# Prompt attention in a two-layer hybrid decoder: eight fill products ahead of the scores, and rotary operands padded with zero rows from 32 to 128

## The reference, cut to what matters

```python
s = (jnp.einsum('bqhr,bkr->bhqk', qa, c_kv) + jnp.einsum('bqhd,bkd->bhqk', qr, k_rope)) * scale
s = jnp.where(k_pos[None, :] <= qp[:, None], s, -jnp.inf)
p = jax.nn.softmax(s, axis=-1)
return jnp.einsum('bhqk,bkr->bqhr', p, c_kv)
```

## Time and profile before

| quantity | value |
|---|---|
| runs of the kernel before | 2146.13, 2148.97, 2151.54 us (median 2148.97) |
| the profiled execution: its own time | 2145.22 us |
| the profiled execution: span of its instructions | 2143.1 us |
| TensorE busy in the span | 1848.7 us, 86% |
| DVE, ACT, POOL busy | 759.5, 350.2, 66.1 us |
| mean granted TensorE clock | 0.911 of full |
| prompt stage of layer 0 | 489.7 to 560.2 us |
| prompt stage of layer 1 | 1544.3 to 1614.8 us |

### The profile page before, as it was taken

The page is one execution under the profiler, slowest core; times in us unless marked ns, Lnnn a source line. Parts: engine busy times, 40 slices in busy tenths (PEclk is TensorE's granted clock), DMA queues, the critical chain, the costliest instruction groups (busy, mean ns, idle before and its releaser), DMA issues. The chain is left out here.

```text
span 2143.1 us, 22565 instructions
## 1 busy us (share of the span) xinstructions
PE 1848.7 (86%) x8114; PEld 1088.9 (51%) x8114; DVE 759.5 (35%) x1560; ACT 350.2 (16%) x524; POOL 66.1 (3%) x68
## 2 busy tenths in 40 slices
PE   4999999889889959988479999997998898599883
PEld 2666657456446634433236666674574475343231
DVE  2243357563223342211324234475631242332113
ACT  1013212141101021110001312122311201211000
POOL 0000000000000001111000000000000000011110
PEclk8999999896999979999779999997979999699996
DMA  7565422323364179999366652223235631999982
GB/s 291 184 228 187 138 93 79 118 72 108 119 216 167 69 315 373 422 423 421 120 267 215 220 176 98 102 79 130 68 109 167 216 122 58 370 418 423 423 350 75
DMA packets 107127, 441.05 MB, mean 206 GB/s; under 512 B 19394, under 2 KB 54498, under 8 KB 79746
## 3 DMA queue, kind: packets, MB, share of 16 engines
q1 hardware_dynamic: 79442, 408.63, 50.4%
q10 hardware_dynamic: 18352, 20.40, 3.0%
q0 software_dynamic: 9216, 10.51, 1.4%
HBM read 433.70 MB, written 28.84 MB: 216 GB/s over the span
## 5 line engine op out<-in xcount | busy, mean ns | idle before, releaser
L367 PE MATMUL ps<-s_proj_and_h,w_in_tiles 128*128 128x320 f32 x1280 | 354.4, 438 | 8.3 <-PEq L203 8.3
L367 PEld LDWEIGHTS ps<-s_proj_and_h,w_in_tiles 128*128 128x128 f32 x1280 | 243.9, 192 | 123.4 <-issue 26.7
L177 PE MATMUL ps<-s_proj_and_h,w_in_tiles 128*128 128x320 f32 x960 | 290.8, 452 | 1.2 <-ACT s_proj_and_h L187 1.2
L2036 PE MATMUL ps<-s_proj_and_h,t_ex_xf 128*64 128x512 f32 x1024 | 244.0, 632 | 32.6 <-DMA s_proj_and_h<-w_gate_up 30.9
L177 PEld LDWEIGHTS ps<-s_proj_and_h,w_in_tiles 128*128 128x128 f32 x960 | 185.0, 198 | 88.4 <-issue 25.8
L2036 PEld LDWEIGHTS ps<-s_proj_and_h,t_ex_xf 128*64 128x64 f32 x1024 | 82.9, 146 | 189.9 <-issue 189.9
L1742 PE MATMUL ps<-s_proj_and_h,w_merge 128*128 128x320 f32 x512 | 138.3, 433 | 3.8 <-PEq L1664 3.8
L1742 PEld LDWEIGHTS ps<-s_proj_and_h,w_merge 128*128 128x128 f32 x512 | 97.1, 190 | 45.1 <-issue 4.9
L2060 PE MATMUL ps<-w_down_slots,t_ex_hf 128*64 128x512 f32 x512 | 116.9, 598 | 2.5 <-DVE t_ex_hf L2107 1.0
L2105 DVE TENSOR_TENSOR t_ex_hid<-t_ex_hid,ps 128x256 f32<-128x256 f32 x32 | 13.5, 421 | 254.4 <-ACT t_ex_hid L2131 254.4
L1972 POOL DMA_INDIRECT rt_h_tm<-h_rows,t_ex_token x32 | 33.9, 1060 | 1635.0 <-DMA h_rows<-rt_h_tm 810.8
(11 more groups left out here) (424 smaller groups left out, 2012.4 us busy)
## 6 DMA issues: line engine op xcount, KB each, us to landing
s_proj_and_h<-w_gate_up SPq DMA_DIRECT2D x64, 2048.0 KB, 29.9
w_in_tiles<-w_in SPq DMA_DIRECT2D x140, 512.0 KB, 3.6
w_down_slots<-w_down SPq DMA_DIRECT2D x64, 1024.0 KB, 30.9
w_mod_panels<-w_mod SPq DMA_DIRECT2D x32, 1024.0 KB, 7.3
page_keys<-pages_k SPq DMA_DIRECT2D x128, 192.0 KB, 3.3
s_proj_and_h<-w_mod SPq DMA_DIRECT2D x16, 1024.0 KB, 12.3
w_merge<-w_branch SPq DMA_DIRECT2D x16, 1024.0 KB, 4.9
page_values<-pages_v ACTq DMA_DIRECT2D x96, 128.0 KB, 2.8
```

The lines of the kernel that those rows point to most:

```text
L177: mm = pe.matmul(K.ps[:, self.BANKS[i % 2], 0:T], self.win[:, j, k, :], K.h[:, k, :], start=(k == 0), stop=(k == KD - 1))
L367: mm = pe.matmul(K.ps[:, n % BANKS, 0:T], win[:, j, k, :], K.h[:, k, :], start=(k == 0), stop=(k == KD - 1))
L2036: mm = pe.matmul(K.ps[rows, GU, :], xf[:, k, rows], K.gate_up[:, j, k, :], start=(k == 0), stop=(k == KD - 1))
```

## The change

Three things are edited.

1. The rotary operands have 128 partitions. `K.krope` is [128, 320] and cleared once at the start of the program by POOL; `A.qr` is [128, 8, 320], and POOL clears its partitions 32 to 127 in the project stage of each layer (two memsets). All writers still write partitions 0 to 31. The rotary products of both attentions now contract over 128 rows, 96 of which are zeros.
2. In the prompt stage the 32 fill products stand at other places: 8 ahead of the first scores and 4 ahead of score(1, 0), fewer behind score(1, 1).
3. ACT's four `F.copy` calls in that stage move accordingly.

```diff
+        @block.gpsimd                                   # in mla_project_stage
+        def _(pool):
+            nc.gpsimd.memset(A.qr[ROPE:2 * ROPE], 0.0)
+            nc.gpsimd.memset(A.qr[2 * ROPE:P], 0.0).then_inc(s("qr_cleared"), 1)
+            pool.wait_ge(s("qr_cleared"), 1)
...
+            F.products(pe, 8)                           # TensorE, mla_prompt_stage
             score(0, 0)
             score(0, 1)
+            F.products(pe, 4)
             score(1, 0)
             turn(0)
             turn(1)
             F.products(pe, 4)
             pe.wait_ge(s("pr_pT_copied"), 2)
             score(1, 1)
             value(0, 0, 0)
+            F.products(pe, 4)
+            value(0, 1, 1)
             F.products(pe, 6)
-            value(0, 1, 1)
-            F.products(pe, 8)
             turn(2)
             turn(3)
-            F.products(pe, 8)
+            F.products(pe, 4)
             value(1, 0, 3)
             turn(4)
             turn(5)
-            F.products(pe, 6)
+            F.products(pe, 2)
             value(1, 1, 5)
...
-        qr_b = K.proj[0:ROPE, XBC0:XBC0 + 2, 0:NB * NSAMP // 2].rearrange("p c (b q) -> p c b q", b=NB // 2)
+        qr_b = K.proj[:, XBC0:XBC0 + 2, 0:NB * NSAMP // 2].rearrange("p c (b q) -> p c b q", b=NB // 2)
...
-                            keys = A.keys[0:P if c < 2 else ROPE, r, HALF * g:HALF * (g + 1), c * P:(c + 1) * P]
+                            keys = A.keys[:, r, HALF * g:HALF * (g + 1), c * P:(c + 1) * P]
...
-        K.krope = sb("krope", [ROPE, T])
+        K.krope = sb("krope", [P, T])
...
+            @block.gpsimd                               # in the first block of the program
+            def _(pool):
+                nc.gpsimd.memset(K.krope[:, :], 0.0).then_inc(once["krope_cleared"], 1)
+                pool.wait_ge(once["krope_cleared"], 1)
...
-                    A.qr = K.proj[0:ROPE, HI0:HI0 + MH, :]
+                    A.qr = K.proj[:, HI0:HI0 + MH, :]
```

More of the change, by code:

```diff
@@ L388, in _ @@
             dve.wait_ge(s("small_done"), 1)
-            v.tensor_copy(K.krope[:, :], K.ps[0:ROPE, SMALL, 0:T])
+            v.tensor_copy(K.krope[0:ROPE, :], K.ps[0:ROPE, SMALL, 0:T])
             v.tensor_copy(K.dt[:, :], K.ps[ROPE:ROPE + NH, SMALL, 0:T]).then_inc(s("dt_copied"), 1)
@@ L1202, in _ @@
             sp.wait_ge(s("krope_ready"), 1)
-            sp.dma_start(K.d["o_krope"][l], K.krope[:, :]).then_inc(s("krope_stored"), 16)
+            sp.dma_start(K.d["o_krope"][l], K.krope[0:ROPE, :]).then_inc(s("krope_stored"), 16)
             F.load(sp, 5)
@@ L1220, in _ @@
             link(v.tensor_tensor(rot[:, 0], K.ps[0:ROPE, 2, 0:T], K.sin[:, :], ALU.mult))
-            link(v.tensor_tensor(K.krope[:, :], K.krope[:, :], K.cos[:, :], ALU.mult))
-            v.tensor_tensor(K.krope[:, :], K.krope[:, :], rot[:, 0], ALU.add).then_inc(s("krope_ready"), 1)
+            link(v.tensor_tensor(K.krope[0:ROPE, :], K.krope[0:ROPE, :], K.cos[:, :], ALU.mult))
+            v.tensor_tensor(K.krope[0:ROPE, :], K.krope[0:ROPE, :], rot[:, 0], ALU.add).then_inc(s("krope_ready"), 1)
             dve.wait_ge(s("ckv_tm"), 1)
@@ L1235, in _ @@
                 v.tensor_copy(qn[:, h % 2], head[0:NOPE]).then_inc(s("q_nope_copied"), 1)
-                v.tensor_tensor(A.qr[:, h], head[NOPE:NOPE + ROPE], K.cos[:, :], ALU.mult)
+                v.tensor_tensor(A.qr[0:ROPE, h], head[NOPE:NOPE + ROPE], K.cos[:, :], ALU.mult)
                 ins = v.tensor_tensor(rot[:, h % 2], head[NOPE + ROPE:P], K.sin_turned[:, :], ALU.mult)
@@ L1240, in _ @@
                 dve.wait_ge(s("q_rope_read"), h + 1)
-                v.tensor_tensor(A.qr[:, h], A.qr[:, h], rot[:, h % 2], ALU.add)
+                v.tensor_tensor(A.qr[0:ROPE, h], A.qr[0:ROPE, h], rot[:, h % 2], ALU.add)
                 if h == 0:
@@ L1287, in _ @@
         def _(pe):
-            pe.matmul(K.ps[0:ROPE, 2, 0:T], K.turn[:, :], K.krope[:, :], start=True, stop=True).then_inc(s("krope_turned"), 1)
+            pe.matmul(K.ps[0:ROPE, 2, 0:T], K.turn[:, :], K.krope[0:ROPE, :], start=True, stop=True).then_inc(s("krope_turned"), 1)
             F.products(pe, 6)
@@ L1475, in copy_output @@
                                ).then_inc(s("pr_o_copied"), 1)
+            F.copy(act)
             exp(0, 0)
@@ L1484, in _ @@
             copy_output(0, 1)
-            F.copy(act)
             copy_turned(2)
@@ L2194, in sb @@
             return ctx.enter_context(nc.sbuf_tensor("s_" + name, shape, dt))
-        once = {n: ctx.enter_context(nc.semaphore(n)) for n in ("consts_loaded", "silu_c_ready")}
+        once = {n: ctx.enter_context(nc.semaphore(n)) for n in ("consts_loaded", "silu_c_ready", "krope_cleared")}
         phase_sems, phase = {}, [ExitStack()]
```

## The result

The changed kernel takes 2100.44 us (median of 4 runs, 2098.23 to 2102.28) against 2147.55 us for the kernel before (4 runs): a ratio of 0.9783, 95% interval 0.9768 to 0.9797. The forecast was 2103 us, 2090 to 2128.

What follows compares the result with a forecast made beforehand. TensorE's own list and its clock were taken to bound the prompt stage. Per layer 48.7 us for 70.4 is -21.7, with the sample stage -23.0, two layers -46: 2149 - 46 = 2103 us, range 2090 to 2128.

Steps and rivals of the forecast that it cites:

- What bounds the stage: First prompt stage: TensorE's own list sets its length, busy 70.4 of 70.5 us; DVE, ACT and page loads don't matter.
- Padding: Prompt scores: units of six evenly spaced 128-row loads take 0.66 us (ends 0.66 and 1.05), 24 units 15.8 us.
- Rival B: Prompt scores: something other than rows makes the gap, units stay at 1.05 us; 2124 us in all, chance 0.11.
- Fill ahead of the scores: Start of prompt stage: fill raises the clock after 4.5 us of low clock, costing 2.3 us (1.3 to 3.2).
- New waits: Prompt stage, TensorE: no wait at turn(2), 8.8 us ahead of it for DVE's 6.2; value(1, 1) waits 0.3 us.
- The stage: Prompt stage, per layer: the terms of TensorE's list sum to 48.7 us for 70.4, so -21.7.
- Memsets, page loads: Project stage: POOL's memsets about 5 us, hidden, taken as 0; prompt stage: SP's page loads still hidden, cover 20 us.
- Sample stage: Sample stage: streamed loads free at most 2.7 us per layer, mostly covered by page loads; gain 1.3, bounds 0 and 2.7.
- Rivals C and D: Clock falls in prompt scores, 2141 us, chance 0.06; or thinned fill behind score(1, 1) lowers the clock stage-long, 2192, chance 0.03.

Runs made afterwards that it cites:

- alternate heads: Fill moved as in the change, no padding, every second head's rotary product first, against the kernel before; 2112.62 us, ratio 0.9846.
- 64 rows: Changed kernel with the prompt scores' rotary products reading 64 rows instead of 128; 2122.61 us, ratio 0.9876 to the kernel before.
- sixteen units with gaps: Kernel before with fill moved, no padding, four fill products moved on so 16 score units form one block; 2123.20 us, one run.
- second set of runs: Changed kernel unedited, run again beside the kernel before on the same chip; 2104.35 us, 5 runs, ratio 0.9808.

## Why the prediction was right, step by step

- *What bounds the stage:* right. It is TensorE's own list; no wait but the 0.3 us one appeared.
- *Padding:* right, and by its reason. Units come at 0.66 to 0.67 us for the 0.66 forecast. Of the two ends the chosen one held. The changed kernel rules out the tensors, alternate heads the 32-row product by itself, and 64 rows the zeros: it is the change of rows. Rival B is out. The rule quoted against it (a load of 32 rows takes as long as one of 128, the Trainium skill, "TensorE: Matmul & The Clock Gate", LDWEIGHTS) fits the single load (0.175 us both) and says nothing of its neighbours. The other rule, a drain on a change of tiling mode (the Trainium skill, "TensorEngine Tiling (Array Packing)", Key Properties), fits the step of 0.19 us at full clock, though no run shows that the step is such a drain.
- *Fill ahead of the scores:* the size was right, the attribution wasn't. The clock was low for 5.5 to 6.0 and 2.7 to 3.2 us, 4.5 were taken. But the prediction put the raised clock down to the fill. The fill does it alone (11.4 us per layer), yet the padded scores do it as well (21.2 alone, 21.4 with both): the two edits overlap, and the second one is worth nothing beside the first. The prediction didn't ask what padding does to the clock.
- *New waits:* turn(2) was expected 2.6 us behind its data and came 2.5 behind; value(1, 1) was to wait 0.3 us and did.
- *The stage:* 48.7 us forecast; TensorE is busy 49.6 and 48.1. The two prompt stages give 42.7 us where 43.4 were forecast.
- *Memsets, page loads:* 2.2 us each for the 2.3 taken from DVE's rate, hidden; the sample stage starts with no wait for pages.
- *Sample stage:* the one term that was mis-sized. 1.3 us per layer was forecast and the two stages show 0.0 in sum. What TensorE was to be freed of is right: two key halves that stream take 5.15 us (581.91 to 587.06), 2.58 each as forecast, and it is busy 2.7 us less per layer (67.1 before, 64.4 after), as the upper bound has it. What failed is the overlap: the first half and the last pair and a half were taken to lie outside the cover of the page loads, but the waits for pages grew by some 2.1 us per layer, most of what was freed. Part of it is that an earlier TensorE asks for value pages while the last key pages are under way, as the kernel with the later value pages shows; how large that part is beside the scatter stays open. The bounds had zero in them.
- *Rivals C and D:* the clock neither fell in the scores nor behind them, and sixteen units with gaps didn't lower it.

The forecast of 2103 lies 2.6 us above the result, and that closeness is in part luck. The stages give 42.7 us for the 46.0 of the sum. The medians are 47.1 apart, more than any stage accounts for; in the second set of runs they are 40.3 apart (2104.35 beside 2144.61). So the stages bear out the mechanism in the prompt stage, and the last few us of the total bear out nothing.

## What to carry to other kernels

Look at the spacing of weight loads, not at their lengths or at the busy share: a TensorE that is "busy" for 70.4 of 70.5 us had 30% of its time (21.4 us) in steps between products of different row counts and in a clock that this list did not raise. Where short contractions stand between full ones, pad them with zeros or put like with like, then ask again what the fill that was to warm the clock is still worth. And read a freed engine's gain only where that engine sets the pace: in the stage that waits for pages the freed 2.7 us per layer turned into waits for pages.

## What the runs showed of the hardware

- A step between fp32 weight loads of 128 and 32 rows costs 0.19 us at 2.4 GHz, either way, and 0.29 at 1.2 GHz (0.58 for two); one from 64 to 128 rows costs 0.19 us at 2.4 GHz as well. Between equal row counts, 32 and 32 included, loads follow each other in 0.11 us at 2.4 GHz.
- The same list of units with gaps kept the clock at 0.50 for 30 us when it started there, and at 1.00 for 17 us when it started there. In these two runs what came before decided which of the two levels it had.
- Under 128-row products without gaps the clock had risen 2.7 to 6.4 us after the stage's start, fill and scores alike.
- POOL's memset took 2.22 us for 2560 columns on 32 partitions and 2.23 on 64; 320 columns on 128 took 0.37, 640 on 64 took 0.63 and 2048 on 64 took 1.80 (the last two in the kernel with the padded project stage). Its time goes by the columns, not by the partitions.
- A stretch that no edit was meant to change came out up to 6 us different between programs: from the end of the first sample stage to the second prompt stage it took 900.3 to 906.3 us. In it only POOL's hidden memsets differ, and in the kernels with the padded project stage that stage.
- TensorE waited 8.7 and 9.5 us for pages in the sample stages of the kernel before and 10.4 to 12.3 in the changed kernel's four, where it had 2.7 us less to do.
